# Two chained transformer blocks on one core: the second block's input products from unscaled activations, the norm's root applied to the products

## What is computed

```
h = concat([meta, x])                                   # 528 x 1024
u = h * rsqrt(mean(h * h) + eps) * norm_mix_pre         # rms_norm, per token
proj = u @ w_in      # dq, dk, dv, dz (512 each), db, da (8 each), aq (512), ak, av (128 each)
o_dn = gated_deltanet(dq, dk, dv, dz, db, da)           # 5-tap conv and silu on dq, dk, dv; chunked delta rule
o_at = axial_gqa(aq, ak, av)                            # rms_norm per head, rotation, softmax over all 528 keys
h = h + rms_norm(concat([o_dn, o_at]) @ w_out) ; then relu^2 feed-forward
```

## Time and profile before

| | us |
|---|---|
| median of 3 runs | 1524.57 (1524.3 to 1526.25) |
| the profiled execution | 1525.86 |
| its span, first to last instruction | 1524.0 |
| PE busy | 1403.7 (92%) |
| DVE busy | 734.2 (48%) |
| ACT busy | 422.1 (28%) |
| POOL busy | 788.4 (52%) |

### The profile page before, as it was taken

One profiled execution on the slowest core, in us unless ns is written; L12 is line 12 of the kernel. 1 busy time (PEld: TensorE's weight loads), 2 busy tenths in 40 slices (PEclk: granted clock), 3 DMA queues, 4 the chain that ended last, 5 costly groups with the idle time before them and its releaser, 6 DMA issues.

```text
span 1524.0 us, 20352 instructions
## 1 busy us (share of the span) xinstructions
PE 1403.7 (92%) x7564; PEld 1149.6 (75%) x7564; DVE 734.2 (48%) x1080; ACT 422.1 (28%) x834; POOL 788.4 (52%) x459
## 2 busy tenths in 40 slices
PE   5789699988999999999898999877998999999996
PEld 3667577767888888788798888657876888888884
DVE  5688545654455546311667887487616111211112
ACT  3123344432221212110344445442423111111111
POOL 4556433336666666666353533314172766666661
PEclk9899989999999999999999999996998999999998
DMA  4222111212232223322121111100021322222221
GB/s 171 69 83 72 67 56 59 66 42 97 99 96 96 96 96 96 97 96 96 56 70 42 56 55 45 42 1 2 1 97 42 111 97 96 97 96 96 97 82 55
DMA packets 31740, 113.87 MB, mean 75 GB/s; under 512 B 3520, under 2 KB 3904, under 8 KB 31424
## 3 DMA queue, kind: packets, MB, share of 16 engines
q1 hardware_dynamic: 31680, 113.03, 22.3%
HBM read 110.92 MB, written 2.10 MB: 74 GB/s over the span
## 4 chain that ended last, share of the span: by engine, by line
PE 82%; DVE 13%; ACT 4%; issue 1%; DMA 0%; DVEq 0%; ACTq 0%
PE ps L997 39%; PE ps L1187 18%; PE ps L1327 6%; ACT arena L537 3%; PE ps L1016 3%; PE ps L1037 2%; PE ps L1030 2%; DVE arena L1657 2%; PE ps L1207 1%; PE ps L1301 1%; PE ps L1139 1%; PE ps L1128 1%; PE ps L1281 1%; PE ps L1090 1%; DVE arena L2064 1%
## 5 line engine op out<-in xcount | busy, mean ns | idle before, releaser
L456 POOL TENSOR_SCALAR w_hi<-raw 128x1024 fp32r<-128x1024 f32 x204 | 221.8, 1087 | 614.8 <-PE ps L997 227.9
L458 POOL TENSOR_TENSOR w_lo<-raw,w_hi 128x1024 fp32r<-128x1024 f32 x204 | 516.7, 2533 | 17.1
L997 PE MATMUL ps<-h_hi,w_hi 128*128 128x512 f32 (+1 forms) x976 | 377.9, 393 | 12.1 <-ACT arena L537 9.8
L997 PE MATMUL ps<-h_lo,w_hi 128*128 128x512 f32 (+1 forms) x976 | 371.1, 386 | 0.0
L997 PE MATMUL ps<-h_hi,w_lo 128*128 128x512 f32 (+1 forms) x976 | 371.0, 385 | 0.0
L997 PEld LDWEIGHTS ps<-h_hi,w_hi 128*128 128x128 f32 x976 | 183.3, 190 | 57.6 <-issue 11.0
L997 PEld LDWEIGHTS ps<-h_lo,w_hi 128*128 128x128 f32 x976 | 183.2, 190 | 37.5 <-issue 2.2
L997 PEld LDWEIGHTS ps<-h_hi,w_lo 128*128 128x128 f32 x976 | 182.8, 190 | 36.3
L537 ACT ACTIVATE arena<-ps 128x512 f32<-128x512 f32 (+7 forms) x213 | 101.2, 508 | 291.7 <-PE ps L997 115.6
L537 ACT ACTIVATE arena<-arena 128x512 f32<-128x512 f32 (+6 forms) x191 | 101.4, 534 | 232.2 <-DVE arena L2212 134.3
L1187 PE MATMUL ps<-g_hi,w_hi 128*128 128x512 f32 x400 | 155.9, 390 | 0.9 <-DVE arena L1825 0.9
(11 more groups left out here) (269 smaller groups left out, 1872.3 us busy)
## 6 DMA issues: line engine op xcount, KB each, us to landing
raw<-in_w_stream SPq DMA_DIRECT2D x204, 512.0 KB, 3.5
xT<-in_x_t SPq DMA_DIRECT2D x2, 1056.0 KB, 6.6
out<-xT SPq DMA_DIRECT2D x8, 256.0 KB, 2.1
C<-in_cst SPq DMA_DIRECT2D x1, 576.0 KB, 9.4
arena<-in_cst SPq DMA_DIRECT2D x1, 528.0 KB, 4.5
arena<-in_pos SPq DMA_DIRECT2D x1, 256.0 KB, 3.9
V<-in_vec SPq DMA_DIRECT2D x1, 174.5 KB, 8.0
band<-in_cst SPq DMA_DIRECT2D x1, 160.5 KB, 3.8
```

The lines of the kernel that those rows point to most:

```text
L456: pool.tensor_scalar(w_hi[j][:], raw[j % 2][:], 1.0, 1.0, ALU.mult, ALU.mult).then_inc(S["pool_step"], 1)
L458: pool.tensor_tensor(w_lo[j][:], raw[j % 2][:], w_hi[j][:], ALU.subtract).then_inc(split_done[j], 1)
L997: last = mm(dst[p], w[:, k, :], h[:, k, cols], start=(k == 0 and n == 0), stop=(k == KT - 1 and n == 2))
```

## The change

- At the join, ACT makes h_hi as xT times the gain, and the square of the tile into a place of its own (SQL, 8 tiles); DVE makes h_lo as xT times the gain less h_hi, directly behind each add. The root is not in them.
- The squares are summed over the eight tiles on DVE (seven adds into n_rs), and PE makes one product with ones, behind the first product pair and ahead of the gates' product, in banks 6 and 7. PE waits there for the adds.
- The root is applied by DVE to each product in PSUM: `scaled2` for the six attention products (written back to PSUM, read by ACT as before), the copy of the gates, and `dn_in` for the 16 products of the delta net, which takes the place of ACT's copy. What is left of `dn_copy` on ACT is the middle tap, `dn_middle`.
- PE starts the pair when the down projection's banks 0 to 3 have been added to xT.

`SUMMED = (1, 2, 3, 4)` lists the norms whose sum PE makes in one product; `parts_before` counts as before.

```diff
@@ -280,6 +280,7 @@
         F2 = arena[:, 0:8 * T].rearrange("p (a b) -> p a b", b=T)
+        SQL = arena[:, 0:KT * L].rearrange("p (a b) -> p a b", b=L)
         bat = n_h[0:16, 0, :]
...
@@ -552,8 +555,8 @@
-                if n in (1, 3, 4):
-                    act.wait_ge(S["sum_done"], (n + 2) // 2)
+                if n in SUMMED:
+                    act.wait_ge(S["sum_done"], SUMMED.index(n) + 1)
                 else:
@@ -718,13 +721,13 @@
                 act.wait_ge(S["x_ready"], 8 + f + 1)
-                square(2, f, xT[:, f, :], L)
+                a(h_hi[:, f, :], xT[:, f, :], ACT.Copy, scale=vcol("mix_pre", f)).then_inc(S["hi_ready"], 1)
+                a(SQL[:, f, :], xT[:, f, :], ACT.Square).then_inc(S["sq_ready"], 1)
             act.wait_ge(S["ba_loaded"], 16)
-            root(2, ps[:, 0:2, 0:HALF], lambda x: x.rearrange("p (a b) -> p a b", a=2))
-            high(3, slice(0, L))
+            root(2, ps[:, 6:8, 0:HALF], lambda x: x.rearrange("p (a b) -> p a b", a=2))
@@ -735,7 +738,7 @@
             def k2_in(t, n, u, gain):
-                product(act, u)
+                act.wait_ge(S["in_scaled"], 0 + n + 1)
@@ -750,10 +753,8 @@
             k2_in(0, 0, U_AT2, vcol("k_norm2"))
-            product(act, U_AT2 + 1)
+            act.wait_ge(S["in_scaled"], 0 + 2)
             a(flat(x5[:, 1, 0:L]), two(1), ACT.Copy).then_inc(S["t2_read"], 1)
-            act.wait_ge(S["ba_rows"], 1)
-            a(bat.rearrange("p (a b) -> p a b", a=2), ps[0:16, 4:6, 0:HALF], ACT.Copy).then_inc(S["bat_ready"], 1)
             act.wait_ge(S["v2_turned"], 1)
@@ -797,18 +798,8 @@
-            def dn_copy(d):
-                product(act, U_DN2 + d)
-                if d == 0:
-                    act.wait_ge(S["k2_dve"], 5)
-                if d >= 12:
-                    a(DZ[:, d - 12, 0:HALF - META], two(0)[:, 0, META:HALF], ACT.Copy)
-                    a(DZ[:, d - 12, HALF - META:T], two(0)[:, 1, :], ACT.Copy).then_inc(S["t2_read"], 1)
-                    return
-                wait(act, S["dn_c"], d - 1)
-                a(flat(x5[:, d % 2, 2:L + 2]), two(0), ACT.Copy).then_inc(S["t2_read"], 1)
+            def dn_middle(d):
                 wait(act, S["dn_c"], d)
@@ -827,9 +818,9 @@
-            dn_copy(0)
             exp2(0)
             exp2(1)
+            dn_middle(0)
             for q in range(16):
@@ -842,7 +833,8 @@
                     exp2(2 * q + 3)
-                    dn_copy(q + 1)
+                if q < 11:
+                    dn_middle(q + 1)
             for d in range(4, 8):
@@ -1217,11 +1209,7 @@
-            pe.wait_ge(S["x_ready"], 10)
-            for f in range(KT):
-                squares(2, f, [ps[:, 0, 0:HALF], ps[:, 1, 0:HALF]], halves)
-            pe.wait_ge(S["rs_ready"], 3)
+            pe.wait_ge(S["x_ready"], 12)
@@ -1244,6 +1232,11 @@
             tile_pair(U_AT2, 3, [two(0), two(1)], halves)
+            pe.wait_ge(S["sq_used"], 24)
+            pe.wait_ge(S["x_ready"], 16)
+            for c in range(2):
+                last = mm(ps[:, 6 + c, 0:HALF], ones[:], n_rs[:, halves[c]], start=True, stop=True)
+            last.then_inc(S["sum_done"], 1)
             pe.wait_ge(S["ba_split"], 3)
@@ -1251,6 +1244,7 @@
             pe.wait_ge(S["t2_read"], 2)
+            pe.wait_ge(S["rs_ready"], 3)
             for b in range(5):
@@ -1851,21 +1845,42 @@
                 v.tensor_tensor(xT[:, f, REAL], xT[:, f, REAL], ps[:, f, :], ALU.add).then_inc(S["x_ready"], 1)
+                dve.wait_ge(S["hi_ready"], parts_before(3) + f + 1)
+                v.scalar_tensor_tensor(out=h_lo[:, f, :], in0=xT[:, f, :], scalar=vcol("mix_pre", f), in1=h_hi[:, f, :],
+                                       op0=ALU.mult, op1=ALU.subtract).then_inc(S["h_ready"], 1)
+            some = cst_ap("ident").unsqueeze(1).to_broadcast([P, KT, P])
+            step(v.tensor_scalar(wba_hi, some, 0.0, None, ALU.mult))
+            v.tensor_scalar(wba_lo, some, 0.0, None, ALU.mult).then_inc(S["ba_split"], 1)
+            for f in range(1, KT):
+                dve.wait_ge(S["sq_ready"], 16 + f + 1)
+                if f > 1:
+                    dve.wait_ge(S["sq_used"], 16 + f)
+                v.tensor_tensor(n_rs, n_rs if f > 1 else SQL[:, 0, :], SQL[:, f, :], ALU.add).then_inc(S["sq_used"], 2 if f == 1 else 1)
+            dve.wait_ge(S["ba_split"], 2)
+            v.tensor_tensor(wba_lo[:, :, 0:16], wba32, wba_hi[:, :, 0:16], ALU.subtract).then_inc(S["ba_split"], 1)
             for n, name in enumerate(("ident", "neg_f", "neg_b")):
             last.then_inc(S["masks_ready"], 1)
-            some = cst_ap("ident").unsqueeze(1).to_broadcast([P, KT, P])
-            step(v.tensor_scalar(wba_hi, some, 0.0, None, ALU.mult))
-            v.tensor_scalar(wba_lo, some, 0.0, None, ALU.mult).then_inc(S["ba_split"], 1)
-            dve.wait_ge(S["ba_split"], 2)
-            v.tensor_tensor(wba_lo[:, :, 0:16], wba32, wba_hi[:, :, 0:16], ALU.subtract).then_inc(S["ba_split"], 1)
             dve.wait_ge(S["rs_ready"], 3)
-            parts(3, slice(0, L), gained("mix_pre", slice(0, L)))
+            def two(n):
+                return ps[:, 2 * (n % 2):2 * (n % 2) + 2, 0:HALF]
                 return x.rearrange("p (a b) -> p a b", a=2)
+            def scaled2(n):
+                product(dve, U_AT2 + n)
+                v.tensor_tensor(two(n), two(n), flat(n_ri), ALU.mult).then_inc(S["in_scaled"], 1)
+            def dn_in(d):
+                product(dve, U_DN2 + d)
+                if d >= 12:
+                    v.tensor_tensor(DZ[:, d - 12, 0:HALF - META], two(0)[:, 0, META:HALF], n_ri[:, META:HALF], ALU.mult)
+                    v.tensor_tensor(DZ[:, d - 12, HALF - META:T], two(0)[:, 1, :], n_ri[:, HALF:L], ALU.mult).then_inc(S["t2_read"], 1)
+                else:
+                    v.tensor_tensor(flat(x5[:, d % 2, 2:L + 2]), two(0), flat(n_ri), ALU.mult).then_inc(S["t2_read"], 1)
@@ -1916,8 +1931,17 @@
+            scaled2(0)
+            scaled2(1)
+            dve.wait_ge(S["ba_rows"], 1)
+            v.tensor_tensor(bat.rearrange("p (a b) -> p a b", a=2), ps[0:16, 4:6, 0:HALF], flat(n_ri[0:16]), ALU.mult
+                            ).then_inc(S["bat_ready"], 1)
             dve.wait_ge(S["c2_loaded"], 16)
             for t in range(5):
+                if t == 1:
+                    scaled2(2)
+                if 1 <= t < 4:
+                    scaled2(t + 2)
                 dve.wait_ge(S["t2_read"], 1 if t == 0 else t + 2)
@@ -1994,6 +2018,7 @@
             for q in range(16):
+                dn_in(q)
                 if q < 12:
```

More of the change, by code:

```diff
@@ L301, in build @@
             "hn_ready hi_ready h_ready x_ready ones_ready "
-            "tile_read rope_ready qk_side qk_sqrt qk_dve kb_done kb_ready v_turned v_ready "
+            "in_scaled tile_read rope_ready qk_side qk_sqrt qk_dve kb_done kb_ready v_turned v_ready "
             "win_ready pg_ready pm_read gp_done "
@@ L340, in normed_before @@
         def normed_before(n):
-            return parts_before(n) - (8 if n > 2 else 0)
+            return parts_before(n) - (16 if n > 3 else 0)
         def product(eng, u, i=0):
@@ L376, in pair @@
             return (2 * p + 1, 2 * p) if d else (2 * p, 2 * p + 1)
+        SUMMED = (1, 2, 3, 4)
         LEVELS = [(0, 8), (1, 0)]
```

## The result

| | before | after |
|---|---|---|
| median, 5 runs each (us) | 1524.45 (1522.64 to 1526.25) | 1532.45 (1530.59 to 1533.22) |
| the profiled execution, its span | 1525.86, 1524.0 | 1532.45, 1530.6 |
| PE, DVE, ACT, POOL busy | 1403.7, 734.2, 422.1, 788.4 | 1398.8, 745.6, 412.0, 791.4 |

The account below looks back on a forecast made before the run. PE was taken as the bound, 82% of the span, with DVE and ACT counting only where PE waits. Terms -0.1 + 2.2 + 4.2 + 2.35 = +8.65, say +8.5, gave 1533.1 us, range 1527.0 to 1540.0.

Parts of the forecast that it names:

- The join's wait: Between the blocks, PE waits for DVE's adds, four meeting POOL; gates' product starts 0.2 us earlier, not 11.8.
- The clock at the join: Behind a PE stand of 10.6 us at the join, PE returns at the lower clock: +2.2 us, ends 1.5 and 2.6.
- The preparation: Before the second attention's loop, DVE's added multiplies, later first delta product and shifted POOL meetings: +4.2 us, ends 1.5 and 5.8.
- shifted meetings: In the preparation, small operations and rotations of queries 2 and 3 meet POOL differently: about 1.0 us more.
- The separate 1.0 for `dn_in`: DVE takes in the first delta product behind normalisations and small tables, so PE starts the second about 1.0 us later.
- The loop: Second attention's loop: products leave PSUM by DVE instead of ACT; +2.35 us, ends 1.2 and 5.
- Ordinary rounds: In the loop, DVE takes 0.70 for ACT's 0.61: 0.1 us later for PE in each of 10 rounds, 1.0.
- The round of decays: Loop round where POOL also prepares the decays: DVE is busy, so the next product starts 1.05 us later.
- Rival 1: The join keeps its gain, low parts and adds not waiting for POOL: -4.6, 1520.0 us; chance 0.05, its half 0.10.
- Rival 2: DVE becomes the loop's bound, its PSUM multiply waiting for POOL's split: rounds 0.5 to 1.0 longer, 1539 to 1545; chance 0.07.
- The estimate by the Trainium skill: At the join, POOL held 0.7 instead of 0.4 at each of four turns, the sum 1.2 us later still.

Follow-up runs that it names:

- copies_on_act: Changed kernel with ACT copying the 16 delta net products again, at its old places, root left out of them: 1532.24 us, ratio 1.0052.
- copies_on_act_late: As copies_on_act on the changed kernel, but with ACT's first copy behind the first two exponentials: 1528.24 us, ratio 1.0027.
- pool_after_adds: Changed kernel with POOL's next two weight splits at the join held until DVE's adds of squares are done: 1527.91 us, ratio 1.0020.
- attn_unscaled: Changed kernel without DVE's six multiplies of the attention products, root left out of q, k and v: 1531.17 us, ratio 1.0043.
- before_held: Kernel before with only POOL's splits for two delta products held until the last query is rotated: 1527.18 us, ratio 1.0017.
- splits_held: On adds_between, POOL's splits for two delta products held until the last query is rotated: 1517.80 us, ratio 0.9954.
- adds_between: Changed kernel with each add of squares between the next residual add and its low part, zero fills behind them: 1522.27 us, ratio 0.9985.
- scaling_moved: On adds_between, multiplies of queries 1 to 3 behind the previous query's rotation, first delta product ahead of the small tables: 1518.07 us, ratio 0.9959.
- gates_first: Changed kernel with the gates' product ahead of the sum products on PE, gates' low part ahead of DVE's adds: 1532.50 us, ratio 1.0054.

## Why the prediction was right

The forecast was 1533.1 us, the measured median 1532.45: the mechanism and its place were those predicted. That the two lie within 0.7 us is in part luck: the sum was +8.65 us, the trace shows +7.18, the medians happen to lie 8.0 apart, and within the preparation and the loop misses of 1 to 1.6 us cancelled. Point by point:

- **The join's wait: right, nearly to the tenth.** Low parts 0, 4 and 5 meet POOL, and no others. The last low part was put at 750.3 and ended 750.06; the last add was put 33.6 us behind the first residual add (762.5 less 728.94) and ended 33.5 behind it. Four adds met POOL and three did not.
- **The clock at the join: 1.4 for 2.2, inside what this place scatters.** The step was to take the price of a pair behind a stand of 4.6 us (ahead of 374.62) for a stand of 10.2. In after it is 1.4: the sum products took 2.12 for 1.1, the gates' product 6.25 for 5.87. With the 0.2 that the product was to start earlier, the join cost +1.2, not +2.1. But the same instructions behind the same stand cost 2.9 in copies_on_act and copies_on_act_late (2.13 and 7.72), and 2.2 in pool_after_adds (2.13 and 7.02), behind a stand of 5.1. So 1.4 is one draw and not the right value of the term; why the clock comes back sooner in one of these kernels than in another stays open.
- **The preparation: +3.8 for +4.2, by misses that cancel.** From the end of the gates' product to the start of the second delta product (813.78 and 818.29, from the first residual add 84.84 and 89.86) it took 3.8 us more. Up to the first maximum 3.2 were forecast (0.75 and 1.4 for multiplies, 1.0 for shifted meetings) and 4.5 measured. The separate 1.0 for `dn_in` behind normalisations and tables was not seen as such: from the first maximum to that product after takes 4.8 us (813.51 to 818.29) and before 5.4, since before had a meeting there of its own. The step that was mis-sized is the adding of multiplies and meetings as separate prices. Without the multiplies (attn_unscaled) 4.3 of the 4.5 us are gone; with the meetings of the two late splits gone from both kernels (before_held, splits_held) the multiplies cost 0.3. Together they cost more because the multiplies use up the idle time under which before had hidden more than half of its meetings (4.7 us of them, of which 2.0 reached the loop).
- **The loop: +2.2 for +2.35, by other parts.** Ordinary rounds +0.1, as predicted. The round of decays +1.06 from the ninth to the eleventh maximum, predicted 1.05. As a whole, copies_on_act puts the price of `dn_in` behind the third maximum at 3.0. Not priced were two changes of the clock: the second product ran at full clock after (3.19 for 4.22, with it the entry got back 1.0), the sixth longer at the lower one (5.51 for 4.43, +1.1). They cancel by chance.
- **Rival 1, that the join keeps its gain**, did not happen, but the gain was there to win: adds_between wins it by another order of DVE's work. The forecast for that gain was 4.6 us in the trace (1520.0); it came out at 2.9 (median 1522.27), because the join gave 9.3 and not 10.1, and the costs behind it were 6.4 and not 5.5. **Rival 2**, DVE as the bound of the loop, is excluded by rounds of 10.13: the multiply from PSUM took 0.72 beside POOL's splits.
- The estimate by the Trainium skill, page "SBUF — State Buffer", section "Who interferes with whom", had POOL held for the whole of DVE's instruction, 0.7 at each turn. POOL's four splits came out 0.48, 0.27, 0.46 and 0.27 longer than alone (1.04, 2.40), so this trace speaks for less than the whole. By the same section DVE is hit where it has two inputs in SBUF or works in a mode with two ports, not otherwise; the trace agrees: the residual adds with one input in PSUM took 0.67 to 0.69 throughout.

The 8.0 us between the medians are 0.8 more than the trace's 7.2; single runs of the kernel before lie up to 3.6 us apart, so that is no difference to explain.

What stays open: how much of a saving in the preparation can be kept. The two arrangements tried keep 2.1 us each at the last maximum, and the third, which holds the splits longest, loses 3.2. A version with the order of scaling_moved and the hold of splits_held was not tried. Why the clock falls at one stretch in one kernel and not in another, in the same code, was not settled.

## What to carry to other kernels

Where DVE and POOL both work from SBUF, as here, a chain of DVE operations can cost what POOL's instructions beside it cost, so put such a chain into gaps that DVE has anyway (here the 0.8 us waits for ACT, 10 us won) and not behind the work that starts POOL. A root that is pulled out of the activations is paid again at each product; count it on the engine that is last there, and expect a saving to shrink at the next place where POOL's work is met. The order of adds_between with either scaling_moved or splits_held takes 0.4% less than before and 0.9% less than after.

## What was not expected

- Size does not help: a 128 by 40 operation that takes 0.20 us alone took 2.28 and 2.33 beside POOL, nearly as much as one of 128 by 528 (2.31 to 2.92).
- Two costs on one engine do not add when one of them lies in idle time: the meetings with the two late splits delay the first maximum by 2.0 us in before and by 6.3 in adds_between, and the multiplies cost 0.3 us without these meetings and 4.5 with them.
- Filling a stand of PE did not remove the lower clock, it moved it: with the stand filled (gates_first) the granted clock was 0.51 from 762 to 772, behind the next, shorter wait; in after it was 0.51 from 755 to 765.
- The sixth delta product, 24 pieces of the same work, took 4.43 us in before, 5.51 in after and 4.50 in scaling_moved, and the second 4.22, 3.19 and 5.13 (before, after, splits_held), according to how much of it ran at the lower clock. Behind the loop, in code that no edit touched, the same made up to 3 us either way, and at the join 1.5 us: the gates' product took 6.25 in after and 7.72 in copies_on_act_late. So single differences of 1 to 1.5 us at such a place are not the edit's own price.
